# A mixture-of-experts stage whose short last blocks are worked out from raw weights, in two column halves

## The chip, the cores and the metric

The kernel runs on one core of a Trainium2 chip. The metric is the device time of one execution, in microseconds (us); less is better.

## What is computed

The reference is one inference step of a small decoder: 1024 prompt tokens and 64 sample tokens go through an mLSTM layer and a latent-attention layer. Each layer ends with the same kind of channel mixer, and only this mixer is touched here. A shared router gives every one of the 1088 tokens two of 16 experts, so 2176 rows are to be worked out per layer:

```
for each expert e, for its rows x (d = 1024):
    hid = silu(x @ w_gate[e]) * (x @ w_up[e])      # 1024 -> 512
    y   = hid @ w_down[e]                          # 512 -> 1024
out[token] += weight * y                           # two rows per token
```

All is float32. The number of rows of an expert depends on the inputs. Run on the given inputs, the reference's own router gives these counts, experts 0 to 15 in order:

```
layer 0: 151 114 183  90 118 163 153 146 167  80  59 164 158  86 170 174
layer 1: 138 120  80  94 144 104  45 129 221 203 227 243 117 109  99 103
```

## The kernel before

The mixer is `stage_experts` (line 1901), run once per layer. Rows are sorted by expert into blocks of 128 rows; each block is a **slot**. An expert with 151 rows has two slots, the second with 23 real rows. That is 26 slots in layer 0 and 23 in layer 1.

*A product.* A float32 product is made of three fp32r products: weights and inputs are split into an upper part (ACT casts, line 2171 for weights, 2182 for x, 2190 for the hidden rows) and a lower part (DVE subtracts, lines 2263, 2277, 2286), and TensorE (PE) adds upper x upper, upper x lower and lower x upper (lines 2083 to 2085). A slot has 24 such matmuls of 512 columns for gate, 24 for up and 24 for down, 8 transposes of its x (`turn_x`, line 2075) and 4 of its hidden rows (`turn_hidden`, line 2111).

*A slot on PE* (`slot(b)`, lines 2124 to 2132): turn the next slot's x, `up(b)`, first half of `gate(b + 1)`, turn the hidden rows of b, second half of `gate(b + 1)`, `down(b)`. ACT and DVE have the same slot in their own order (lines 2201 to 2216 and 2288 to 2298): on ACT the four pieces of the next gate matrix come first, then the store of the slot before (two copies of PSUM, a drain, one DMA of 512 KB, lines 2192 to 2199), then the two halves of x with two pieces of down after each, the hidden rows, and four pieces of up around silu.

*Weights.* Each matrix (2 MB) has one raw buffer; `load` (line 2010) on the SP queue waits until DVE has lowered the last piece of what was there, then fetches the next. A slot of the same expert as the slot before loads nothing: a table `slot_fresh`, made by DVE in `tables` (line 2420), tells so, and ACT and DVE skip their casts and subtractions (`renew`, lines 2173 and 2266). So 16 times three matrices are loaded per layer. Loads are issued in the order down(b + 1), up(b + 2), gate(b + 3).

*Rows* are gathered by POOL with an indirect DMA into one buffer `xg` (line 2051), which is free again when PE has turned it.

*Loops.* Each engine runs `slots` (line 1994): a loop over all 31 slots that there could be beside the last, with an If that jumps over the body when the slot is not used. The last slot stands behind the loop. Ahead of it DVE works out choices, counts, destinations and tables (lines 2303 to 2434) while PE counts with triangular matmuls (lines 2139 and 2149).

The stage before stores the rows `h2` and fills the part of `yrows` that might stay unwritten (line 1641). The stage after (`stage_combine_latents`, or `stage_combine` in layer 1) gathers `yrows`. The residual rows `g.x` stay in SBUF meanwhile.

The structure that sets the order is the SP queue, with this part of the code:

```
def load(z, b):
    with sp.If(table(sp, g.slot_fresh, b) > 0):
        e = table(sp, g.slot_expert, b) + layer * E
        sp.wait_ge(s_lo[z], b * PIECES + PIECES)
        fetch(z, e)
```

## Time and profile before

| | us |
|---|---|
| median of 3 runs (2448.67 to 2456.14) | 2454.08 |
| the profiled execution, its own time | 2450.45 |
| its span | 2448.8 |
| PE busy in the span | 2236.8 (91%) |
| granted TensorE clock, mean | 0.958 |
| slots of layer 0, from the first slot's start to the last's | 700.8 to 1144.7 |
| slots of layer 1, likewise | 1962.8 to 2355.7 |

The span is taken from the trace of one execution; what lies around it is 1.65 us. A time such as 700.8 counts from the span's start. Busy shares are averages over stages with different limits, so the rows further down are read by stretch: who starts when, and what the row says it waited for (the releaser, behind "<-").

### The profile page before, as it was taken

The numbers are of one execution on the slowest core, as the hardware profiler recorded it, in microseconds if no ns is written. First come the engines' busy times: TensorE is split into PE (matmuls) and PEld (weight loads), VectorE is DVE, ScalarE is ACT, GpSimd is POOL, SyncE is SP. The second block draws the span as 40 slices with busy tenths as digits, with TensorE's granted clock in tenths as the row PEclk, the third lists the DMA queues.
The fourth block names the chain that finished last, engine by engine and source line by source line (L and its number), as shares of the span: only waits on it lengthen the run. The fifth ranks groups of instructions, "written<-read, shape, count | busy, mean of one in ns | idle before, by whom it ended". The sixth has DMA issues, their size and how long they took to land. (4 is left out here: it accounts for less than half of the span.)

```text
span 2448.8 us, 39160 instructions
## 1 busy us (share of the span) xinstructions
PE 2236.8 (91%) x11590; PEld 1675.6 (68%) x11590; DVE 1332.6 (54%) x2251; ACT 1098.1 (45%) x1870; POOL 305.4 (12%) x387
## 2 busy tenths in 40 slices
PE   7999997889689999999799999999989599999974
PEld 4766665667578888887486565656678487888852
DVE  4222312586766756663783444433357677755657
ACT  3211212553346655663543344434332356755645
POOL 0000001670010000000100433000000010000103
PEclk8999998899889999999899999999999699999986
DMA  7566655665468778784556544333351388866956
GB/s 283 173 213 213 218 202 161 173 209 199 157 210 301 289 257 286 275 302 171 156 169 198 180 147 141 94 99 97 101 216 44 128 295 322 325 244 223 328 203 230
DMA packets 194323, 503.98 MB, mean 206 GB/s; under 512 B 19152, under 2 KB 39089, under 8 KB 187696
## 3 DMA queue, kind: packets, MB, share of 16 engines
q1 hardware_dynamic: 165902, 409.88, 49.0%
q0 software_dynamic: 18416, 64.11, 7.4%
q10 hardware_dynamic: 9906, 28.75, 3.3%
q8 instruction: 53, 0.87, 0.1%
q14 instruction: 46, 0.38, 0.0%
HBM read 437.13 MB, written 73.42 MB: 208 GB/s over the span
## 5 line engine op out<-in xcount | busy, mean ns | idle before, releaser
L2263 DVE TENSOR_TENSOR e_wl<-e_raw_gate_up,e_wh 128x1024 fp32r<-128x1024 f32 x256 | 299.7, 1223 | 97.3 <-ACT e_wh L2171 96.5
L2083 PE MATMUL e_psG<-e_wh,e_xh 128*128 128x512 f32 x784 | 315.9, 403 | 11.6 <-issue 7.6
L2085 PE MATMUL e_psG<-e_wh,e_xl 128*128 128x512 f32 x784 | 307.1, 392 | 0.0
L2084 PE MATMUL e_psG<-e_wl,e_xh 128*128 128x512 f32 x784 | 306.2, 391 | 0.0
L2171 ACT CAST e_wh<-e_raw_gate_up 128x1024 fp32r<-128x1024 f32 x256 | 251.2, 1046 | 80.0 <-DMA e_raw_gate_up<-in_e_up 25.3
L2083 PEld LDWEIGHTS e_psG<-e_wh,e_xh 128*128 128x128 f32 x784 | 147.7, 188 | 42.1 <-issue 10.3
L2085 PEld LDWEIGHTS e_psG<-e_wh,e_xl 128*128 128x128 f32 x784 | 147.4, 188 | 32.2
L2084 PEld LDWEIGHTS e_psG<-e_wl,e_xh 128*128 128x128 f32 x784 | 148.0, 189 | 28.3
L2263 DVE TENSOR_TENSOR e_wl<-e_raw_down,e_wh 128x1024 fp32r<-128x1024 f32 x128 | 153.2, 1219 | 15.1 <-ACT e_wh L2171 15.1
L615 PE MATMUL in_ps<-in_w_upper,in_h_upper 128*128 128x512 f32 x384 | 155.5, 405 | 3.1 <-DVE in_h_lower L335 2.7
L2083 PE MATMUL e_psY<-e_wh,e_hh 128*128 128x512 f32 x392 | 154.3, 394 | 2.8 <-DVE e_hl L2286 2.8
L2084 PE MATMUL e_psY<-e_wl,e_hh 128*128 128x512 f32 x392 | 153.7, 392 | 0.0
L2085 PE MATMUL e_psY<-e_wh,e_hl 128*128 128x512 f32 x392 | 153.6, 392 | 0.0
L616 PE MATMUL in_ps<-in_w_lower,in_h_upper 128*128 128x512 f32 x384 | 150.7, 393 | 0.0
L617 PE MATMUL in_ps<-in_w_upper,in_h_lower 128*128 128x512 f32 x384 | 150.4, 392 | 0.0
L2171 ACT CAST e_wh<-e_raw_down 128x1024 fp32r<-128x1024 f32 x128 | 128.1, 1051 | 1.6 <-DMA e_raw_down<-in_e_down 1.6
L2277 DVE TENSOR_TENSOR e_xl<-e_psX,e_xh 128x512 fp32r<-128x512 f32 x98 | 67.2, 688 | 111.0 <-ACT e_xh L2182 111.0
L2182 ACT CAST e_xh<-e_psX 128x512 fp32r<-128x512 f32 x98 | 57.4, 588 | 152.5 <-PE e_psG L2085 123.7
L742 ACT ACTIVATE in_out<-in_ps 128x512 f32<-128x512 f32 (+1 forms) x54 | 32.2, 597 | 206.4 <-PE in_ps L617 201.8
L300 DVE TENSOR_TENSOR in_w_lower<-in_w_raw,in_w_upper 128x512 fp32r<-128x512 f32 x40 | 27.7, 692 | 173.2 <-ACT in_w_upper L294 172.4
L3640 ACT COPY x<-a_psP 128x512 f32<-128x512 f32 (+3 forms) x112 | 52.3, 497 | 127.0 <-PE a_psP L3487 117.0
L1664 PE MATMUL o_ps<-o_w_halves,o_mix_halves 128*128 128x512 f32 (+1 forms) x256 | 102.6, 401 | 3.3 <-DVE o_w_halves L1871 2.2
(616 smaller groups left out, 4490.2 us busy)
## 6 DMA issues: line engine op xcount, KB each, us to landing
e_raw_gate_up<-in_e_gate SPq DMA_DIRECT2D x32, 2048.0 KB, 11.7
e_raw_gate_up<-in_e_up SPq DMA_DIRECT2D x32, 2048.0 KB, 9.3
e_raw_down<-in_e_down SPq DMA_DIRECT2D x32, 2048.0 KB, 7.9
x<-in_ada_w SPq DMA_DIRECT2D x40, 1024.0 KB, 5.4
yrows<-e_y ACTq DMA_DIRECT2D x49, 512.0 KB, 6.7
x<-in_cache SPq DMA_DIRECT2D x64, 320.0 KB
a_pages<-in_cache SPq DMA_DIRECT2D x64, 320.0 KB, 3.5
qkvo<-in_out SPq DMA_DIRECT2D x48, 256.0 KB, 2.3
```

The lines of the kernel that those rows point to most:

```text
L615: T.matmul(dst, up, high[:, k, :], start=(k == 0), stop=False)
L616: T.matmul(dst, up, low[:, k, :], start=False, stop=False)
L617: mm = T.matmul(dst, lw, high[:, k, :], start=False, stop=(k == KD - 1))
L1664: T.matmul(dst, up, wh[k][:, cols], start=(k == 0), stop=False)
L2083: T.matmul(out, upper[:, k, :], wh[:, z, cols], start=k == 0, stop=False)
L2084: T.matmul(out, upper[:, k, :], wl[:, z, cols], start=False, stop=False)
L2085: mm = T.matmul(out, lower[:, k, :], wh[:, z, cols], start=False, stop=k == PIECES * n - 1)
L2171: S.copy(wh[:, z, c * PC:(c + 1) * PC], raw[z][:, c * PC:(c + 1) * PC]).then_inc(s_hi[z], 1)
L2182: S.copy(xh[:, half * 4:half * 4 + 4, :], psX[:, half * 4:half * 4 + 4, :]).then_inc(s_xh, 1)
L2263: V.tensor_tensor(wl[:, z, at], raw[z][:, at], wh[:, z, at].bitcast(F32), ALU.subtract).then_inc(s_lo[z], 1)
L2277: V.tensor_tensor(xl[at], psX[at], xh[at].bitcast(F32), ALU.subtract).then_inc(s_xl, 1)
L3640: S.copy(pT[:, par, lo:hi, :], psP[:, lo:hi, :])
```

## The change

- A slot counts as one only if it has more than 64 rows, or is its expert's first. An expert's last 1 to 64 rows beyond that are a **rest**. For the counts above: 16 slots and 10 rests in layer 0 (experts 0, 2, 5, 6, 7, 8, 11, 12, 14, 15), 20 slots and 3 rests in layer 1 (experts 0, 4, 7). The rest of an expert is worked out beside its last slot.
- A rest's products are plain float32 matmuls that read the raw weights: 64 rows stand as the stationary operand, and the two halves of the output's columns go to the two halves of the PSUM partitions. Gate and up: 8 pairs of matmuls of 256 columns each; down: 4 pairs of 512 columns. There are also 8 transposes of 64 rows of x and 2 of the hidden rows.
- So a raw buffer is also held until the rest's product with it is done: `load` waits for `s_rest[z]`. The gate product of a rest stands in the middle of the down products of the slot before, its up product behind the slot's up, its down product behind the slot's down.
- All slots load weights: `slot_fresh` and the skipping are gone, and the second slot of an expert (four of them, all in layer 1) loads its matrices again. The issue order is gate(b + 1), down(b), up(b + 1).
- A rest's rows are gathered into the same `xg`; the gather of the next slot's x waits until the rest's x is turned. Its result is stored by four DMAs.
- The buffers of a rest lie over the sample rows of `g.x`, which are parked in DRAM and fetched back by the next stage, and over the triangle constants.
- DVE's routing has some more steps, and the tables are made ahead of the token numbers instead of behind them. The loops run over 30 slots. More of `yrows` is filled in the stage before.

The diff, cut to its core:

```diff
-SLOTS = (2 * N + E * (P - 1)) // P
-FULL = 2 * N // P
-
+ROWS = P // 2
+SLOTS = E + (2 * N - 3 * (ROWS + 1)) // P
+PLACES = SLOTS + E + 1
...
-                first = FULL + 2 * t
-                if layer == 0 and first < SLOTS:
-                    more = min(2, SLOTS - first) * P
+                first = E + FILL * t
+                if layer == 0 and first < PLACES:
+                    more = min(FILL, PLACES - first) * P
...
+        parked = g.x[:, PT, :]
+        xr = parked[:, 0:KD * ROWS].rearrange("p (k t) -> p k t", k=KD)
+        hidr, hr = parked[:, HALF:HALF + FE // 2], parked[:, HALF + FE // 2:D]
+        yr = [nc.alloc_sbuf_tensor_at(f"e{layer}_y_rest", [P, FE // 2], F32, offset=g.tri_at), hr]
...
+        psR = ctx.enter_context(nc.psum_tensor(f"e{layer}_psR", [P, 2, FE // 2], F32))
...
+        def rests(eng, b, n):
+
+            return [table(eng, g.slot_halves, b + j) for j in range(n + 1)]
+
+        def with_rest(eng, count, next_count, work):
+
+            with eng.If(next_count > count):
+                work(count)
+            with eng.Else():
+                eng.sem_inc(s_end, 1)
...
             def load(z, b):
-                with sp.If(table(sp, g.slot_fresh, b) > 0):
-                    e = table(sp, g.slot_expert, b) + layer * E
-                    sp.wait_ge(s_lo[z], b * PIECES + PIECES)
-                    fetch(z, e)
-                with sp.Else():
-                    sp.wait_ge(s_raw[z], b * 16)
-                    sp.sem_inc(s_raw[z], 16)
-                sp.drain()
+                e = table(sp, g.slot_expert, b) + layer * E
+                count = table(sp, g.slot_halves, b)
+                sp.wait_ge(s_rest[z], count)
+                sp.sem_inc(s_end, 1)
+                sp.wait_ge(s_lo[z], b * PIECES + PIECES)
+                fetch(z, e)
...
+            used = table(sp, g.slots_used, 0)
+            with sp.Fori(1, SLOTS - 1) as b:
+                with sp.If(used > b + 1):
+                    load(GATE, b + 1)
+                    load(DOWN, b)
+                    load(UP, b + 1)
+                with sp.Else():
+                    sp.sem_inc(s_end, 1)
+            load(DOWN, used - 1)
...
+            def gather_rest(b, h):
+                take(h + (SLOTS - 1), 1)
+                po.wait_ge(s_xt, b + 1)
+                po.sem_inc(s_end, 1)
+                nc.gpsimd.indirect_dma_start(xg[0:ROWS, :], None, g.h2, bass.IndirectOffsetOnAxis(tok[0:ROWS, 1:2], axis=0)
+                                             ).then_inc(s_rx, 16)
...
+                po.wait_ge(s_rt, mine)
+                po.sem_inc(s_ask, 1)
+                gather(tok[:, 0:1])
+                with_rest(po, mine, after, lambda h: gather_rest(b + 1, h))
...
+            def turn_rest(h):
+                pe.wait_ge(s_rx, 16 * h)
+                pe.sem_inc(s_end, 1)
+                for k in range(KD):
+                    mm = T.transpose(psX[:, k, 0:ROWS], xg[0:ROWS, k * P:(k + 1) * P], g.ident[0:ROWS, 0:ROWS])
+                mm.then_inc(s_rt, 1)
+
+            def rest_product(z):
+                for k in range(KD):
+                    for r, c in zip(sides(ROWS), sides(FE // 2)):
+                        mm = T.matmul(psR[r, z, :], xr[:, k, :], raw[z][:, k * FE + c.start:k * FE + c.stop],
+                                      start=(k == 0), stop=(k == KD - 1))
+                mm.then_inc(s_rest[z], 1)
+
+            def gate_rest(h, stored):
+                pe.wait_ge(s_rout, stored)
+                pe.sem_inc(s_end, 1)
+                pe.wait_ge(s_rhf, h)
+                pe.sem_inc(s_end, 1)
+                pe.wait_ge(s_rxf, h)
+                rest_product(GATE)
+
+            def up_rest(h):
+                pe.wait_ge(s_rsilu, h + 1)
+                pe.sem_inc(s_end, 1)
+                pe.wait_ge(s_rout, h)
+                rest_product(UP)
+
+            def turn_rest_hidden(h):
+                pe.wait_ge(s_rhid, h)
+                for j in range(2):
+                    mm = T.transpose(psR[:, 1, j * P:(j + 1) * P], hidr[:, j * P:(j + 1) * P], g.ident[:])
+                mm.then_inc(s_rht, 1)
+
+            def down_rest(h, gates):
+                pe.wait_ge(s_rsilu, gates)
+                pe.sem_inc(s_end, 1)
+                pe.wait_ge(s_rhf, h + 1)
+                out = psR[:].rearrange("p z f -> p (z f)")
+                for f in range(FT):
+                    at = f % 2 * P + f // 2 * ROWS
+                    for r, c in zip(sides(ROWS), sides(HALF)):
+                        mm = T.matmul(out[r, :], hr[:, at:at + ROWS], raw[DOWN][:, f * D + c.start:f * D + c.stop],
+                                      start=(f == 0), stop=(f == FT - 1))
+                mm.then_inc(s_rest[DOWN], 1)
...
             def slot(b):
+                here, soon, later = rests(pe, b, 2)
                 pe.wait_ge(s_xl, b * 2 + 2)
                 turn_x(b + 1)
                 up(b)
+                with_rest(pe, here, soon, up_rest)
                 pe.wait_ge(s_silu, b + 1)
                 gate(b + 1, 0)
                 turn_hidden(b)
+                with_rest(pe, here, soon, turn_rest_hidden)
                 gate(b + 1, 1)
-                down(b)
+                with_rest(pe, soon, later, turn_rest)
+                down(b, range(2))
+                with_rest(pe, soon, later, lambda h: gate_rest(h, here))
+                down(b, range(2, PIECES))
+                with_rest(pe, here, soon, lambda h: down_rest(h, later))
...
+            first = rests(pe, 0, 1)
+            with_rest(pe, *first, turn_rest)
+            with_rest(pe, *first, lambda h: gate_rest(h, h))
...
+            def copy_rest(h):
+                act.wait_ge(s_rt, h + 1)
+                S.copy(xr, psX[:, :, 0:ROWS]).then_inc(s_rxf, 1)
+
+            def silu_rest(h):
+                act.wait_ge(s_rest[GATE], h + 1)
+                S.activation(hidr, psR[:, 0, :], ACT.Silu).then_inc(s_rsilu, 1)
+
+            def copy_rest_hidden(h):
+                act.wait_ge(s_rst, 64 * h)
+                act.sem_inc(s_end, 1)
+                act.wait_ge(s_rht, h)
+                S.copy(hr, psR[:, 1, :]).then_inc(s_rhf, 1)
+
+            def store_rest(h):
+                act.wait_ge(s_rest[DOWN], h + 1)
+                for j in range(2):
+                    S.copy(yr[j][:, :], psR[:, j, :])
+                act.drain()
+                act.sem_inc(s_rout, 1)
+                for z in range(2):
+                    for j in range(2):
+                        at = z * HALF + j * (HALF // 2)
+                        act.dma_start(g.yrows[bass.ds((h + (SLOTS - 1)) * P, ROWS), at:at + HALF // 2],
+                                      yr[j][z * ROWS:(z + 1) * ROWS, :]).then_inc(s_rst, 16)
...
             def slot(b, first=False):
-                now, soon = (table(act, g.slot_fresh, b + j) for j in range(2))
-                renew(GATE, b + 1, soon, b + 1)
+                here, soon, later = rests(act, b, 2)
+                renew(GATE, b + 1, b + 1)
                 if not first:
                     store(b - 1)
                 act.wait_ge(s_xt, b + 2)
                 act.wait_ge(s_xu, b + 1)
                 copy_x(0)
-                renew(DOWN, b, now, b + 1, range(2))
+                renew(DOWN, b, b + 1, range(2))
                 act.wait_ge(s_used[UP], b + 1)
                 copy_x(1)
-                renew(DOWN, b, now, b + 1, range(2, PIECES))
+                renew(DOWN, b, b + 1, range(2, PIECES))
                 copy_hidden(b)
-                renew(UP, b + 1, soon, b + 1, range(2))
+                with_rest(act, here, soon, copy_rest_hidden)
+                renew(UP, b + 1, b + 1, range(2))
                 silu(b + 1)
-                renew(UP, b + 1, soon, b + 1, range(2, PIECES))
+                with_rest(act, soon, later, copy_rest)
+                renew(UP, b + 1, b + 1, range(2, PIECES))
+                with_rest(act, soon, later, silu_rest)
+                with_rest(act, here, soon, store_rest)
...
+            def multiply_rest(h):
+                v.wait_ge(s_rsilu, h + 1)
+                v.sem_inc(s_end, 1)
+                v.wait_ge(s_rest[UP], h + 1)
+                V.tensor_tensor(hidr, hidr, psR[:, 1, :], ALU.mult).then_inc(s_rhid, 1)
+
             def slot(b):
-                now, soon = (table(v, g.slot_fresh, b + j) for j in range(2))
-                renew(GATE, b + 1, soon)
+                here, soon = rests(v, b, 1)
+                lower(GATE, b + 1)
                 lower_x(b + 1, 0)
-                renew(DOWN, b, now, range(1))
+                lower(DOWN, b, range(1))
                 multiply(b)
                 lower_x(b + 1, 1)
-                renew(DOWN, b, now, range(1, 3))
+                lower(DOWN, b, range(1, 3))
+                with_rest(v, here, soon, multiply_rest)
                 lower_hidden(b)
-                renew(DOWN, b, now, range(3, PIECES))
-                renew(UP, b + 1, soon)
+                lower(DOWN, b, range(3, PIECES))
+                lower(UP, b + 1)
...
+                V.tensor_tensor(summed[:], upto[:], rest[:].unsqueeze(1).broadcast_to([P, E, E]), ALU.mult)
+                v.drain()
+                V.tensor_reduce(shift[:], summed[:], AX, ALU.add)
                 V.scalar_tensor_tensor(out=place[:], in0=tmp[:].unsqueeze(1).broadcast_to(sh3), scalar=float(P),
                                        in1=counted, op0=ALU.mult, op1=ALU.add)
                 v.drain()
+                V.scalar_tensor_tensor(out=shift[:], in0=shift[:], scalar=float(SLOTS - 1), in1=ends[:],
+                                       op0=ALU.add, op1=ALU.subtract)
+                V.tensor_tensor(over[:], counted, room[:].unsqueeze(1).broadcast_to(sh3), ALU.is_ge)
+                v.drain()
+                V.scalar_tensor_tensor(out=over[:], in0=over[:], scalar=float(P),
+                                       in1=shift[:].unsqueeze(1).broadcast_to(sh3), op0=ALU.mult, op1=ALU.mult)
+                v.drain()
+                V.tensor_tensor(place[:], place[:], over[:], ALU.add)
...
+            tables()
             v.wait_ge(s_num, 1)
-            V.tensor_scalar(tokens[:], psH[:, 0, 0:SLOTS], float(N), None, ALU.add).then_inc(s_tok, 1)
-            V.tensor_tensor(full[:], ends[:].unsqueeze(1).broadcast_to([P, TABLE, E]),
-                            g.count_up[:].unsqueeze(2).broadcast_to([P, TABLE, E]), ALU.is_le)
-            v.drain()
-            V.tensor_reduce(slotf[:], full[:], AX, ALU.add)
-            v.drain()
-            tables()
+            V.tensor_scalar(tokens[:], psH[:, 0, 0:PLACES], float(N), None, ALU.add).then_inc(s_tok, 1)
```

## Rows read from the trace of the kernel before

**Rows 1.** The page, engines over the span: busy us (share) xinstructions

```profile
PE 2236.8 (91%) x11590; PEld 1675.6 (68%) x11590; DVE 1332.6 (54%) x2251; ACT 1098.1 (45%) x1870; POOL 305.4 (12%) x387
```

**Rows 2.** Stores of slots in ACT's queue, layer 0 and layer 1: duration ns, first and last start

```profile
L2199 ACTq DMA_DIRECT2D yrows<-e_y x26: 343/348/414, 720.8 to 1164.6; - x26
...
L2199 ACTq DMA_DIRECT2D yrows<-e_y x23: 338/343/377, 1982.8 to 2379.8; - x23
```

**Rows 3.** Timeline of PE: start us, us, engine, line [idle before <-releaser]

```profile
700.82 1.03 PE L2075 MATMUL e_psX<-c_ident,e_xg 128*128 128x128 f32 x8
...
718.54 1.03 PE L2075 MATMUL e_psX<-c_ident,e_xg 128*128 128x128 f32 x8
...
1147.21 0.49 PE L2083 MATMUL e_psG<-e_wh,e_xh 128*128 128x512 f32 x1 [2.47 <-issue]
...
1962.81 1.03 PE L2075 MATMUL e_psX<-c_ident,e_xg 128*128 128x128 f32 x8
...
2360.90 0.79 PE L2083 MATMUL e_psG<-e_wh,e_xh 128*128 128x512 f32 x1 [5.16 <-issue]
```

**Rows 4.** Timeline of a fresh slot of layer 1 with fresh neighbours, same columns

```profile
2034.59 1.03 PE L2075 MATMUL e_psX<-c_ident,e_xg 128*128 128x128 f32 x8
2034.97 3.89 ACT L2171 CAST e_wh<-e_raw_gate_up 128x1024 fp32r<-128x1024 f32 x4 [1.00 <-DMA e_raw_gate_up<-in_e_gate]
2040.56 0.59 ACT L2182 CAST e_xh<-e_psX 128x512 fp32r<-128x512 f32 x1 [0.73 <-issue]
2041.18 0.69 DVE L2277 TENSOR_TENSOR e_xl<-e_psX,e_xh 128x512 fp32r<-128x512 f32 x1 [0.18 <-ACT e_xh L2182]
2044.46 2.35 DVE L2263 TENSOR_TENSOR e_wl<-e_raw_down,e_wh 128x1024 fp32r<-128x1024 f32 x2
...
2053.52 1.03 PE L2075 MATMUL e_psX<-c_ident,e_xg 128*128 128x128 f32 x8
```

**Rows 5.** Busy us by engine in 2010 to 2040, then PE clock, DMA share, GB/s

```profile
2010.00:2040.00 30.00, 29.38 (x139) 24.14 (x139) 25.22 (x25) 23.93 (x29) 4.51 (x4) 1.00 1.03 389
```

**Rows 6.** The page, issues of weights: count, KB each, median us to landing

```profile
e_raw_gate_up<-in_e_gate SPq DMA_DIRECT2D x32, 2048.0 KB, 11.7
e_raw_down<-in_e_down SPq DMA_DIRECT2D x32, 2048.0 KB, 7.9
```

**Rows 7.** Timeline of PE in attention, float32 pairs with 64 stationary columns

```profile
1317.57 0.38 PE L3370 MATMUL a_psP<-x,cq_sample 128*64 128x256 f32 x1
1317.79 0.38 PE L3370 MATMUL a_psP<-x,cq_sample 128*64 128x256 f32 x1
...
1693.71 2.80 PE L3461 MATMUL a_psS<-x,a_q_pair 128*64 128x512 f32 x12
1696.44 0.33 PE L3487 MATMUL a_psP<-c_ident,x 128*128 128x128 f32 x1
```

**Rows 8.** ACT between two slots of one expert: timeline, then its queue's table loads

```profile
769.05 1.05 ACT L2171 CAST e_wh<-e_raw_gate_up 128x1024 fp32r<-128x1024 f32 x1 [2.00 <-issue]
...
L1986 ACTq TENSOR_LOAD <-slot_fresh x2: 277/288/299, 767.7 to 768.3; - x2
```

**Rows 9.** PE's queue at skipped slots of the loop: ns, first and last start

```profile
L1998 PEldq COMPARE_BRANCH  x2: 214/214/214, 2354.9 to 2355.8; - x2
```

**Rows 10.** Timeline of POOL, gathers without and with other transfers

```profile
694.66 0.98 POOL L2051 DMA_INDIRECT e_xg<-h,e_tok  x1 [1.60 <-PE e_psX L2075]
699.05 1.05 POOL L2060 COPY e_tok<-e_tokens 128x1 int32 x1 [3.41 <-DMA e_xg<-h,e_tok]
...
2045.49 0.23 POOL L2060 COPY e_tok<-e_tokens 128x1 int32 x1 [7.05 <-DMA e_xg<-h,e_tok]
```

**Rows 11.** Timeline of DVE in the routing of layer 0

```profile
676.47 0.42 DVE L2386 TENSOR_TENSOR e_summed<-e_upto,e_blocks 128x256 f32<-128x256 f32 x1
687.47 0.19 DVE L2444 TENSOR_SCALAR e_tokens<-e_psH 128x32 int32<-128x32 f32 x1 [2.84 <-PE e_psH L2149]
687.58 0.73 DVE L2445 TENSOR_TENSOR e_full<-e_ends,c_count_up 128x560 f32<-128x560 f32 x1
```

More of the change, by code:

```diff
@@ L2244, in _ @@
             last = used - 1
[L2245 to L2249 removed]
+            here, soon = rests(act, last, 1)
+            store(used - 2)
+            renew(DOWN, last, last + 1)
             copy_hidden(last)
+            with_rest(act, here, soon, copy_rest_hidden)
             store(last)
+            with_rest(act, here, soon, store_rest)
+            act.wait_ge(s_rst, soon * 64)
+            act.sem_inc(s_end, 1)
             act.wait_ge(s_st, used * 16 + 32)
@@ L2323, in tables_of_counts @@
                 v.drain()
-                V.memset(least[:, 0, 0:1], -1.0)
             def choose():
@@ L2461, in _ @@
             last = table(v, g.slots_used, 0) - 1
-            renew(DOWN, last, table(v, g.slot_fresh, last))
+            here, soon = rests(v, last, 1)
+            lower(DOWN, last)
             multiply(last)
+            with_rest(v, here, soon, multiply_rest)
             lower_hidden(last)
```

138 lines of the change are left out of this document (81 added, 57 removed).

## The prediction, made before the change was run

> **What bounds the kernel now.** First the page: PE is busy in 91% of the span, every other engine far less [rows 1]. Then the stage itself. ACT's queue stores 26 slots in layer 0 and 23 in layer 1 [rows 2]; the same numbers come out of the reference's counts, rounded up to blocks of 128, so the counts hold here. From slot to slot PE takes 718.54 - 700.82 = 17.72 us [rows 3]. This is 72 matmuls and 12 transposes without a gap: 8 transposes take 1.03, some 0.8 without the modelled tail of the last, 4 take 0.4, two changes between kinds 0.2, and 16.3 / 72 = 0.227 is left for a matmul, 2.7 for half a gate product. From the first slot's start to the end of the last down product but one, layer 0 takes 1147.21 - 2.47 - 700.82 = 443.9 and layer 1 takes 2360.90 - 5.16 - 1962.81 = 392.9.
>
> What is next behind PE shows where three slots with new weights (fresh slots, by the table's name) follow each other: a slot there takes 2053.52 - 2034.59 = 18.93, because gate's raw weights landed late (ACT waited 1.00 for the DMA), and the lower half of x, which PE needs, comes 2041.18 + 0.69 - 2034.97 = 6.9 after ACT's first cast of gate [rows 4]. The DMA engines are then full, at 389 GB/s [rows 5]. A fresh slot moves three matrices of 2.10 MB and two times 0.52 MB of rows, 7.34 MB; 7.34 / 389 is 18.9 us. So a slot costs 17.7 by PE and 18.9 by DMA once all are fresh.
>
> **What goes and what comes, on PE.** 49 slots become 36, and 13 rests come. A rest's pairs run side by side in this trace: the same shape of 256 columns steps by 1317.79 - 1317.57 = 0.22 per pair, and 12 matmuls of 512 columns are followed by the next instruction after 1696.44 - 1693.71 = 2.73, or 0.455 for a pair with the change of shape in it [rows 7]. So gate 8 x 0.22 and 0.2 for a change of shape = 2.0, up 2.0, down 4 x 0.455 = 1.8 and 0.2 = 2.0, x's transposes 1.1, hidden ones 0.3: 7.4 us. If that were all, a slot saved (17.7) would be paid with 7.4.
>
> **What it adds as waits.** A rest holds raw buffers that were free early. I count in time from PE's start of a slot.
>
> Gate's matrix for slot b + 1 is asked for when the rest's gate product of b is done. That product is followed by half a down, 2.7, so it is asked for at -2.7, and a matrix takes 7.9 to land when little else is under way [rows 6]: 5.2. Where slot b - 1 had a rest of its own, the request is earlier by its down product, 2.0, but ACT is late: store_rest waits for that product, copies two times 256 columns (0.35 each, estimated from 0.59 for 512 [rows 4]) and drains, 1.0 with the wait, and issues four DMAs, 0.35 each by [rows 2] and some 0.1 of address work, 1.7; then the loop's end and two table loads take 2.00, and a third load one step of 0.6 more, 767.7 to 768.3 [rows 8], less 0.3 of the drain counted before. Sum 5.0. So in both cases gate's casts begin at about 5.1 instead of 0.4, and half of x is ready at 5.0 + 6.9 = 11.9. PE, done with turn, up and up_rest at 0.8 + 5.4 + 2.0 = 8.2, waits 3.7. Half a gate, 14.6; hidden transposes, 15.0. The rest's hidden rows wait on DVE, where multiply_rest is queued behind three pieces of down: 2044.46 + 2.35 - 2034.97 = 11.8 after the first cast [rows 4], plus 0.5: 17.4. Transposed 17.7, second half of gate 20.4, down 5.4, down_rest 2.0: **27.8** for a slot with a rest. With a rest in the next slot too, 1.1 and 2.0 more: **30.9**. A slot without a rest behind one with: 11.9 + 2.7 + 0.4 + 2.7 + 5.4 = **23.1**, and **26.2** if the next has one. A slot without a rest ahead of one with: 17.7 + 3.1 = 20.8, and 1.0 for the next x: its gather now starts only after turn_rest and takes 4.4 alone (694.66 to 699.05), 7.05 and its issue beside other transfers [rows 10]: **21.8**. Anything else: **18.9**.
>
> Behind ACT's four DMA issues are queued gate's casts, store(b - 1) and x's copies; SP's queue is in order, so down(b) and up(b + 1) are late with gate, but down lands at about 10.8, just ahead of its casts, and up is needed later. They cost nothing unless gate gets earlier; then down is late next.
>
> **The sum.** Layer 0, 15 slots ahead of the last: five of 30.9, four of 27.8, two of 26.2, two of 21.8, two of 23.1 = 407.9, against 443.9: -36.0. Layer 1, 19 slots: three of 27.8, three of 23.1, two of 21.8, eleven of 18.9 = 404.2, against 392.9: +11.3. That layer saves only three slots, and the four second slots load again.
>
> Ahead of slot 0, in both layers a slot with a rest: x's gather starts at 701.9, behind turn_rest, and takes 4.7; the slot begins at 706.6, not 700.82: +5.8 each, 11.6.
>
> The end of the loop: a skipped slot costs PE 0.92, 2354.9 to 2355.8 [rows 9]; 6 are skipped in layer 0 now and 9 in layer 1, of which 2.47 and 5.16 are seen as idle [rows 3]. It becomes 15 and 11, as PE's queue is ahead by no more than now: +8.3 and +1.8. In layer 0's last slot come 2.0 of down_rest and 1.1 of its store and other rest work (up_rest stands where PE waits anyway): +3.1. Together 13.2.
>
> Routing: a second product and sum over 256 columns, 0.42 each [rows 11], and four small steps with drains, 1.5; the token table over 48 instead of 32 places, 576 more columns at the 0.73 / 560 of [rows 11], 0.75; the tables, 4.1 in all (two old and two new passes of 0.73 and 1.2 of small steps), move ahead of the token numbers, where 2.84 were idle: 1.3. Sum 4.4 per layer, 8.8. What DVE saves behind the tokens is hidden by the gather. Other edits: the larger fill, the parked rows and their return run beside work, 1 us in all, between 0 and 4 (a 2 MB transfer ends the stage before later if its cover is gone).
>
> Sum: -36.0 + 11.3 + 11.6 + 13.2 + 8.8 + 1 = **+9.9**. From the execution's own 2450.45 that is 2460.4; the median of the runs is 3.6 above that execution, so I say 2464. The bounds of the price taken at least surely, gate's first cast: between 3.4 (ACT's queue runs ahead of its copies) and 9 (a landing of 11.7, the median of gate's loads [rows 6], behind a rest). It acts in 19 slots: -32 to, in the nine with a landing to wait for, +35.
>
> **The Trainium skill against a row.** The rows show 389 GB/s over 30 us. The Trainium skill's page "DMA: Bandwidth & Descriptors", section "Where 436 GB/s comes from", says that between HBM and SBUF about 358 GB/s is the limit. By that, a fresh slot would be 20.5 us, an estimate from the page, and the sum some 18 higher. The trace disagrees with it for this stretch; the sum goes by the row.
>
> **The rivals.**
> A, not slower: gate's casts begin early enough. The point is 5.1 - 9.9 / 19 = 4.6: from there down the change wins. At 2.7, which holds if ACT's loads and DMA issues overlap what it waits for and gate lands at once, it is -2.4 x 19 = -46 and 2418. For it: ACT's queue does run ahead where it is not held (casts of up and gate follow each other). Against: it is held here by a wait and a drain. 0.30.
> B: eleven fresh slots in a row don't keep 389 GB/s, which the trace shows for 30 us only. At a tenth less, 1.9 x 11 = 21: 2485. Against: rate and pitch agree in [rows 4, 5]. 0.10.
> C: jumps. A skipped slot takes 0.92, of which two compares are 0.43 [rows 9]. PE's slot body grows by more than half and has six Ifs; where its queue has lost its lead after a wait, 0.5 to 0.9 could stand open in each of 34 slots: +24 and 2488. Against: 25 returns in layer 0 show no gap now. 0.07. The Trainium skill's page "Runtime: NRT & Kernel Launch", section "Instruction fetch mechanics", says that a taken branch out of the fetched window stalls the sequencer for a fetch; the 0.92 agrees with it.
> D: the pairs go one after the other: 5.4 for each of 13 rests, +70, 2534. The pairs in [rows 7] speak against it. 0.03.
> E, it doesn't do what it says (another number of rests, weights not loaded): the counts match [rows 2], so this is nearly nothing and has no chance of its own.
>
> **The numbers.** The forecast, waits as worked out, has 0.50 and spans 2446 to 2490. A measurement of this kernel can tell about 0.3%, 7 us, from no change: 0.15 of the forecast's 0.50 and a little of A lie within it. Faster 0.29, same 0.17, slower 0.54. The range takes in most of A's better side and B and C: 2415 to 2500.
>
> **What would show it.** Slots of about 31, 28, 26, 23 and 19 us in PE's timeline; gate's first cast at 5 us in slots with a rest or behind one, and PE waiting for DVE's x (line 2277) and then for multiply_rest; pairs at 0.22; DMA at 1.0 and 389 GB/s in the second half of layer 1; a gap near 11 us ahead of layer 0's last slot; routing longer by 4.4. Wrong if casts of gate begin before 4.6, if rest slots take 25, or if fresh slots leave 18.9.

## The result and the profile after

The changed kernel takes 2562.59 us (median of four runs, 2556.92 to 2564.43), the kernel before 2454.93 beside it: 1.044 times as long, interval 1.0423 to 1.0456. So the sign of the forecast was right and its size far off: 2464 with a range up to 2500.

The profiled execution has a span of 2561.2 us, 112.4 more. The page of the changed kernel, PE's busy time and the granted clock in 40 slices:

```profile
span 2561.2 us, 39115 instructions
PE 2212.0 (86%) x11668; PEld 1586.4 (62%) x11669; DVE 1358.6 (53%) x2270; ACT 1121.2 (44%) x1905; POOL 311.3 (12%) x388
PEclk9999998999689999998899999999999689899987
```

PE is busy for 86% of the span where it was 91% [rows 1]: PE now waits. PE's groups of the raw products in the changed kernel (count; busy, mean; idle time before):

```profile
L2167 PE MATMUL e_psR<-e_raw_gate_up,x 128*64 128x256 f32 x832 | 98.9, 392 | 3.9 <-ACT x L2309 3.9
```

There are 13 rests, as worked out. But 832 records are 64 for each, and the code writes 32 matmuls for gate and up together. Each float32 matmul shows as two records.

One slot with a rest, in layer 0, PE's timeline (start, duration, engine, line, operation, in brackets the idle time before it and what ended it):

```profile
969.59 1.09 PE L2120 MATMUL e_psX<-c_ident,e_xg 128*128 128x128 f32 x8
...
976.10 3.67 PE L2167 MATMUL e_psR<-e_raw_gate_up,x 128*64 128x256 f32 x32
982.96 0.49 PE L2128 MATMUL e_psG<-e_wh,e_xh 128*128 128x512 f32 x1 [3.18 <-DVE e_xl L2412]
983.29 0.40 PE L2129 MATMUL e_psG<-e_wl,e_xh 128*128 128x512 f32 x1
...
984.24 0.63 PE L2129 MATMUL e_psG<-e_wl,e_xh 128*128 128x512 f32 x1
984.67 0.63 PE L2130 MATMUL e_psG<-e_wh,e_xl 128*128 128x512 f32 x1
...
987.39 0.60 PE L2206 MATMUL e_psH<-c_ident,e_hid 128*128 128x128 f32 x4
988.15 0.44 PE L2188 MATMUL e_psR<-c_ident,x 128*128 128x128 f32 x2 [0.16 <-DVE x L2427]
...
996.97 3.65 PE L2199 MATMUL e_psR<-e_raw_down,x 128*64 128x512 f32 x16
1000.55 1.09 PE L2120 MATMUL e_psX<-c_ident,e_xg 128*128 128x128 f32 x8
```

A raw product takes 3.6 us, not 2.0. PE waits for the lower half of x, as forecast; behind the wait the pitch of matmuls is 984.67 - 984.24 = 0.43 instead of the 0.227 worked out from [rows 3], so half a gate product takes 987.39 - 982.96 = 4.43 us instead of 2.7. The granted clock of this stretch is 0.62 on average (982.9 to 987.4 us): most of it went at the lower of the clock's two levels (1.2 GHz), and before it PE had stood for 3.18 us. The slot takes 31.0 where the forecast said 27.8.

ACT in the changed kernel: gate's casts of four slots (those that start at 714.51, 781.89, 969.59 and 1000.55), then a rest's stores and gate's first cast around the start of the slot at 898.62.

```profile
725.61 3.88 ACT L2281 CAST e_wh<-e_raw_gate_up 128x1024 fp32r<-128x1024 f32 x4 [10.60 <-DMA e_raw_gate_up<-in_e_gate]
...
788.51 3.89 ACT L2281 CAST e_wh<-e_raw_gate_up 128x1024 fp32r<-128x1024 f32 x4 [8.97 <-DMA e_raw_gate_up<-in_e_gate]
...
975.96 3.89 ACT L2281 CAST e_wh<-e_raw_gate_up 128x1024 fp32r<-128x1024 f32 x4 [5.61 <-issue]
...
1006.77 3.89 ACT L2281 CAST e_wh<-e_raw_gate_up 128x1024 fp32r<-128x1024 f32 x4 [5.46 <-issue]
```
```profile
898.74 0.37 ACT L2324 COPY e_y_rest<-e_psR 128x256 f32<-128x256 f32 x1 [6.14 <-PE e_psR L2199]
899.01 0.38 ACT L2324 COPY x<-e_psR 128x256 f32<-128x256 f32 x1
899.63 0.52 ACTq L2330 DMA_DIRECT2D yrows<-e_y_rest  x1
900.33 0.48 ACTq L2330 DMA_DIRECT2D yrows<-x  x1
900.98 0.53 ACTq L2330 DMA_DIRECT2D yrows<-e_y_rest  x1
901.66 0.55 ACTq L2330 DMA_DIRECT2D yrows<-x  x1
904.78 1.99 ACT L2281 CAST e_wh<-e_raw_gate_up 128x1024 fp32r<-128x1024 f32 x2 [5.39 <-issue]
```

Gate's first cast comes 11.1, 6.6, 6.4, 6.2 and 904.78 - 898.62 = 6.2 us behind the slot's start; the forecast said 5.1. In the first two the load came last, in the others ACT's own issues. A DMA issue is followed by the next after 0.65 to 0.70 here, not 0.45.

The second half of layer 1, ten slots in a row with neither a rest nor one before them, ran as forecast or better (the eleventh such slot stands earlier in the layer). Nine of the ten lie in 2279 to 2445 us of the changed kernel; its engines and DMA there (columns: PE, PEld, DVE, ACT, POOL busy, clock, DMA share, GB/s); [rows 5] is its like:

```profile
2279.00:2445.00 166.00, 161.91 (x758) 132.00 (x757) 147.84 (x144) 130.62 (x162) 20.98 (x17) 1.00 1.03 394
```

Slots of 17.7 to 18.9 us and 394 GB/s. Where the 112.4 us lie, from slot starts in PE's timeline, with the forecast in brackets: slots +26.8 in layer 0 (-36.0) and +32.4 in layer 1 (+11.3); ahead of the first slots +13.7 and +14.6 (10.7 each, with 4.4 of routing and half of the 1 us of other edits); behind the last slot but one +20.1 (11.4) and +4.8 (1.8). So 83.9 of the miss of 102.5 lie in slots.

### The profile page after: what moved, and what is told of

The parts are those of the page before. It is cut to its first block and busy times, and to the rows that moved or that the text cites. A ratio compares the mean times of both kernels' runs of the same rounds, so it can differ in the third digit from the quotient of the medians.

```text
span 2561.2 us, 39115 instructions
## 1 busy us (share of the span) xinstructions
PE 2212.0 (86%) x11668; PEld 1586.4 (62%) x11669; DVE 1358.6 (53%) x2270; ACT 1121.2 (44%) x1905; POOL 311.3 (12%) x388
## 5 line engine op out<-in xcount | busy, mean ns | idle before, releaser
L2406 DVE TENSOR_TENSOR e_wl<-e_raw_gate_up,e_wh 128x1024 fp32r<-128x1024 f32 x288 | 336.0, 1221 | 296.7 <-ACT e_wh L2281 296.3
L2281 ACT CAST e_wh<-e_raw_gate_up 128x1024 fp32r<-128x1024 f32 x288 | 283.4, 1045 | 215.3 <-DMA e_raw_gate_up<-in_e_gate 101.6
L2128 PE MATMUL e_psG<-e_wh,e_xh 128*128 128x512 f32 x576 | 252.4, 438 | 123.0 <-DVE e_xl L2412 99.9
L2129 PE MATMUL e_psG<-e_wl,e_xh 128*128 128x512 f32 x576 | 241.5, 419 | 0.0
L2130 PE MATMUL e_psG<-e_wh,e_xl 128*128 128x512 f32 x576 | 240.6, 418 | 0.0
L2128 PE MATMUL e_psY<-e_wh,e_hh 128*128 128x512 f32 x288 | 114.9, 399 | 2.4 <-DVE e_hl L2421 2.4
L2130 PE MATMUL e_psY<-e_wh,e_hl 128*128 128x512 f32 x288 | 112.3, 390 | 0.0
L2129 PE MATMUL e_psY<-e_wl,e_hh 128*128 128x512 f32 x288 | 112.2, 390 | 0.0
L615 PEld LDWEIGHTS in_ps<-in_w_upper,in_h_upper 128*128 128x128 f32 x384 | 72.4, 189 | 48.5 <-ACT in_out L742 23.2
L2167 PE MATMUL e_psR<-e_raw_gate_up,x 128*64 128x256 f32 x832 | 98.9, 392 | 3.9 <-ACT x L2309 3.9
```

What stands on the lines that cost most here:

```text
L615: T.matmul(dst, up, high[:, k, :], start=(k == 0), stop=False)
L2128: T.matmul(out, upper[:, k, :], wh[:, z, cols], start=k == 0, stop=False)
L2129: T.matmul(out, upper[:, k, :], wl[:, z, cols], start=False, stop=False)
L2130: mm = T.matmul(out, lower[:, k, :], wh[:, z, cols], start=False, stop=k == PIECES * n - 1)
L2167: mm = T.matmul(psR[r, z, :], xr[:, k, :], raw[z][:, k * FE + c.start:k * FE + c.stop], start=(k == 0), stop=(k == KD - 1))
L2281: S.copy(wh[:, z, c * PC:(c + 1) * PC], raw[z][:, c * PC:(c + 1) * PC]).then_inc(s_hi[z], 1)
```

## The experiments

Two theories at first. **T**: the rest's products cost PE twice what I took. **W**: what was mis-sized are the waits, buffers held and ACT late, and the products matter little. Each run is set against 2562; the kernel before, beside them, had medians of 2450 to 2455.

**Price of a rest as a whole** (the last rows of 13 experts are left out):

```
-V.tensor_scalar(g.slot_halves[:], restf[:], 1.0, None, ALU.add)
+V.tensor_scalar(g.slot_halves[:], restf[:], 0.0, 1.0, ALU.mult, ALU.add)
```

> The changed kernel with the table of rests set to 1 everywhere, so that no slot does any rest work on any engine; the last rows of 13 experts are left out. Slots (36), loads, the loop's end and the routing stay. Both theories: what is left are 34 slots at 17.7 (PE) to 18.9 us (DMA) plus heads and tails, so about 2561 - 13 x 22 = 2275 us. It tells the price of one rest with all that it drags along: I expect (2561 - this) / 13 = 22 us, against the 12 us of PE work by theory T (a float32 product is two passes) and about 10 of waits. If the slots stay above 20 us without rests, both theories are wrong and it is the loads of all slots or the new branches.

Measured: 2276.19 us. By the spans, (2561.2 - 2276.8) / 13 = 21.9 us for a rest. Its engines and DMA over ten slots of layer 0:

```profile
785.00:966.00 181.00, 179.24 (x838) 145.86 (x837) 163.75 (x161) 146.60 (x180) 20.10 (x19) 1.00 1.04 403
```

Ten slots in 181.86 us (785.09 to 966.95) at 403 GB/s: loading in every slot costs 0.5 us of a slot and no more. Within the slots, then, neither the branches nor the loads are the cause.

The run says one thing more. The kernel before has a span of 2448.8; less 13 slots of 17.72 it would be 2218.4, and this run's is 2276.8. So 58 us of the 112 come with the change even where no rest is worked out: some 29 in the 34 slots (0.5 in most, 5.8 and 6.7 in the layers' first), 15 in gaps ahead of the two last slots (13.14 and 9.54 where there were 2.47 and 5.16), the remainder ahead of the first slots and in the next stage. The other 54 are 13 times the difference between 21.9 and 17.7.

**Half of each product** (half of the contraction is left out), and **one side of each pair** (all of the right half but its first matmul is left out):

```
-for k in range(KD):          # and f in range(FT) in down_rest
+for k in range(KD // 2):     # and f in range(FT // 2)
```
```
-for r, c in zip(sides(ROWS), sides(FE // 2)):   # in down_rest likewise
+for r, c in list(zip(sides(ROWS), sides(FE // 2)))[:1 if k else 2]:
```

> The changed kernel with each of the rest's three products over half of its contraction (the other half is left out): 16 instead of 32 records in gate_rest and up_rest, 8 instead of 16 in down_rest. Theory T (PE's own work: 3.65 us each, gate_rest and down_rest in full on the path, up_rest where PE waits for x anyway, and raw buffers asked for earlier): 1.8 + 1.8 = 3.6 us less per rest, 13 rests, -47 us: about 2515. Theory W (the cost is that ACT comes late with gate's casts behind store_rest and that raw buffers are held; the products themselves fill time that PE would wait): under 15 us less, 2547 or more.

> The changed kernel with the right-hand column half of each rest's product left out but for its first matmul (so half of each result is wrong); the left-hand half is whole. If the two matmuls of a pair run side by side, each group takes as long as before (gate_rest 3.6, down_rest 3.6 us) and the time stays within 5 us of 2561. If they go one after the other (rival D), the products halve as in the run with half the contraction and the time falls by about 47 us. Theory T says side by side, two passes each: 32 records become about 18, with the same 0.22 us per step.

Measured: 2499.43 us and 2564.87 us. The PE records of line 2167 (gate's and up's raw products) from 700 to 1185 us, first the changed kernel, then one side left out, then half the contraction:

```profile
L2167 PE MATMUL e_psR<-e_raw_gate_up,x 128*64 128x256 f32 x608 | 71.5, 389 | 2.1 <-ACT x L2309 2.1
```
```profile
L2167 PE MATMUL e_psR<-e_raw_gate_up,x 128*64 128x256 f32 x342 | 71.4, 391 | 2.1 <-ACT x L2309 2.1
```
```profile
L2167 PE MATMUL e_psR<-e_raw_gate_up,x 128*64 128x256 f32 x320 | 39.8, 392 | 2.6 <-ACT x L2309 2.5
```

342 records take as long as 608, and 320 over half the contraction take 56% of it. So the two matmuls of a pair do run side by side (rival D is out), and a step of the contraction costs two records of 0.22 us one after the other, called two passes here. Half the products gave 63 us, 4.9 per rest, where T said 3.6 and W at most 15 us in all.

**Next to no products** (all steps of the contraction but the first are left out):

```
-for k in range(KD):
+for k in range(1):           # and f in range(1)
```

> The changed kernel with each of the rest's products cut to its first step of the contraction (one pair for gate and up, one pair for down; the other seven and three are left out). Everything else of a rest stays: gathers, transposes, copies, silu, the four stores, all waits and branches, and raw buffers held until the products are done. Half of the contraction gave 62 us. Theory T: going on to an eighth and a quarter takes another 3.6 x 3/8 x 2 (gate and up, the latter only where PE doesn't wait for x) and 3.6 / 4 for down: 2.2 to 3.6 per rest, and a little more because gate's matrix is asked for earlier: 2455 to 2465. What then still lies between this run and the 2276 without rests, some 180 us or 14 per rest, is waits and fixed work, which would be more than the products. If it falls to 2400 or less, the products are nearly the whole price.

Measured: 2474.98 us, 88 less than 2562 and still 199 above the kernel without rests: 15.3 us a rest that are not its products. That was more than I expected, and T alone falls with it. In this run PE waited longer instead (5.7 to 6.2 us for x in slots with a rest next to others, where it was 3.0 to 4.0): part of the products stood in time that PE would wait.

**ACT's stores later**: store_rest of slot b - 1 behind gate's casts in slot b (and likewise in the last slot).

```
 renew(GATE, b + 1, b + 1)
 if not first:
+    with_rest(act, table(act, g.slot_halves, b - 1), here, store_rest)
     store(b - 1)
...
 with_rest(act, soon, later, silu_rest)
-with_rest(act, here, soon, store_rest)
```

> The changed kernel with ACT's store_rest (wait for down_rest, two copies, drain, four DMA issues) moved from the end of its slot to behind gate's casts of the next one, beside the store of the whole rows. Theory W: gate's first cast behind a rest comes at 3 us or less after the slot's start where it came at 6 (unless the load itself is late), the wait of PE for x shrinks by 3 in up to 12 slots: about -30 us, 2532. Theory T: the same mechanism, but it is the smaller part of the miss; where the load is what comes last (gate asked for only after gate_rest) nothing is won, so -15 to -30. If nothing changes, ACT's place for store_rest doesn't set the pace.

Measured: 2543.07 us, -19.5. A slot behind one with a rest, with no rest of its own and none in the next, falls from 26.4 to 27.0 us to between 23.8 and 25.3, since gate's casts no longer wait for ACT. Where a rest follows a rest nothing is won, but not because the load comes last. Gate's first cast there does come 3.3 to 3.6 us earlier, 2.8 to 3.0 behind the slot's start where it was 6.2 to 6.4, and the load is what it waits for. But the stores now stand between gate's casts and x's. ACT in the slot that starts at 965.30, and x's cast in the changed kernel's slot that starts at 969.59:

```profile
968.10 3.89 ACT L2281 CAST e_wh<-e_raw_gate_up 128x1024 fp32r<-128x1024 f32 x4 [8.82 <-DMA e_raw_gate_up<-in_e_gate]
...
977.31 0.59 ACT L2288 CAST e_xh<-e_psX 128x512 fp32r<-128x512 f32 x1 [0.70 <-issue]
```
```profile
981.51 0.58 ACT L2288 CAST e_xh<-e_psX 128x512 fp32r<-128x512 f32 x1 [0.70 <-issue]
```

x's cast comes 12.0 behind the slot's start, and 11.9 in the changed kernel: ACT has the same work ahead of it in either order.

**Gate's raw product earlier**, ahead of down, or behind its first quarter, both with the late store:

```
-down(b, range(2))
+down(b, range(1))            # in the first of the two: not at all
 with_rest(pe, soon, later, lambda h: gate_rest(h, here))
-down(b, range(2, PIECES))
+down(b, range(1, PIECES))
```

> The changed kernel with store_rest late as in the run before (2543) and gate_rest ahead of the whole down product instead of in its middle. Gate's matrix is asked for 2.7 us earlier, so that less of its landing is waited for: where the load came last, gate's casts come up to 2.7 earlier (-15 to -25 over some 10 slots). Against that, PE meets gate_rest before ACT has copied the rest's rows: 1.4 to 2.1 us open in 13 rests, +18 to +27. So about the same as the late store alone, 2543 within 12. Theory W expects a clear gain, 2520 or less, theory T that the 12 us of PE work per rest stand whatever the order.

> As the run before it, but gate_rest behind the first quarter of down (1.36 us) instead of ahead of it or in its middle: the copy of the rest's rows is covered for the most part, and the load is asked for 1.4 us earlier than in the changed kernel. Both theories: a little better than the late store alone (2543), by 5 to 15: 2532.

Measured: 2537.12 (2532.56 to 2538.79) and 2537.99 (2529.82 to 2540.29): the same as each other, 5 to 6 better than the late store alone.

**Skipped slots** cut off (loops to 19, for these counts only), on the changed kernel and on the last order:

```
-with eng.Fori(0, SLOTS - 1) as b:     # SP's and ACT's own loops likewise
+with eng.Fori(0, 19) as b:
```

> The changed kernel with its loops over slots ending at 19 instead of 30 (enough for the 16 and 20 slots of these inputs only), so 11 skipped slots fewer in each layer: 4 are left in layer 0, none in layer 1. With 0.92 us for a skipped slot on PE, and idle of 13.32 us in layer 0 and 9.59 us in layer 1 ahead of the last slot in the changed kernel's trace: at most 10.1 + 9.6 = 20 us less, 2542; at least 10 less if ACT's or SP's skipped slots end later than PE's anyway. If the gap stays, it wasn't the skipped slots.

> The kernel of the run before it with loops that end at 19: the sum of both, 2532 - 20 = 2512. If theory T is right, no order of these pieces comes near the kernel before (2452): 2276 without rests and 13 x 12 us of PE work alone are 2432, and each rest still drags some us of waiting. Below 2470 would say that the waits were the main part.

Measured: 2549.57, -13 (expected -20), and 2519.8, -18. The gap ahead of the last slot falls from 13.32 to 3.48 us in layer 0 and from 9.59 to nothing in layer 1, where PE then waits 3.75 instead of 0.86 us for DVE's hidden rows. That is 16.5 of gaps, of which the run won 13; where the other 3.5 went isn't shown. 11 iterations fewer took 9.84 off layer 0's gap, 0.89 each.

**A rest's store DMAs issued by SP** instead of ACT, between the loads of down and up, on top of the run before (2519.8):

```
-act.dma_start(g.yrows[...], yr[j][...]).then_inc(s_rst, 16)
...
 load(DOWN, b)
+with_rest(sp, *rests(sp, b - 1, 1), store_rest)
 load(UP, b + 1)
```

> The kernel with the late store, gate_rest behind a quarter of down and loops to 19 (2520), with the four store DMAs of a rest issued by SP between the loads of down and up instead of by ACT. ACT gets 2.6 to 3.2 us back between gate's casts and the copy of x in 12 slots behind a rest; PE waits there for x for 2.2 us and runs its next 9 matmuls at half its clock, 1.7 us. So -2 to -4 in 12 slots, -24 to -48: 2484. The kernel before stands at 2452 to 2455. Theory T: not below it, since the products and 36 slots alone are 2432 and the ends of the layers and the first slots add waits. If it does come below, the design pays once the waits are gone.

Measured: 2532.79, 13 worse, not 24 to 48 better. The slots take as long as before: from the first slot's start to the start of the last one in the loop, layer 0 takes 419.0 us where it took 420.0 in the run before (2519.8), and layer 1 395.2 where it took 395.1. ACT's time is not free to win there, since with its issues gone it came to the casts of down before the load had landed, and waited for it 11 times, 32.8 us together in layer 0, where it had waited 7 times, 19.0 us. The loss lies behind layer 0. SP's queue is in order, and the next stage's first transfers now stand behind the last rest's stores. SP's first transfer and PE's first product with weights of that stage, in the run before and in this one:

```profile
1185.11 0.36 SPq L2072 DMA_DIRECT2D l_rows<-in_ln_g  x1
...
1207.17 1.27 PE L2960 MATMUL l_psL<-l_raw,l_bias 128*33 128x320 f32 x2 [1.52 <-DVEq L3158]
```
```profile
1206.81 0.36 SPq L2083 DMA_DIRECT2D l_rows<-in_ln_g  x1
...
1224.38 1.25 PE L2966 MATMUL l_psL<-l_raw,l_bias 128*33 128x320 f32 x2 [9.95 <-DMA l_raw<-in_w_kv_a]
```

The transfers start 21.7 later, PE 17.2. Of the 12.2 us by which the spans differ, 10.5 lie between the start of the last slot in layer 0's loop and layer 1's first slot. So the 13 us are the price of the new place of the last stores, not of the slots; the run was not repeated with these left on ACT.

**The clock.** In nearly all slots with a rest or behind one, the half gate product behind PE's wait takes 4.4 to 5.3 us. Ten identity matmuls (`keep_warm`) fill the wait in slots with a rest:

```
 rest_product(UP)
+keep_warm(T, g, psH[:, 0, 0:P], 10)
```

> The changed kernel with ten 128 x 128 matmuls of the identity behind the rest's up product, on a bank nobody reads then, and nothing else: PE does them where it waits for x's lower half in the 12 slots that have a rest (waits of 2.96 to 4.0, and 7.4 and 6.0 in the first slot of a layer). Six such took 0.83 us as x6 records for three matmuls, so ten are about 2.8. Theory C2 (the clock): the half gate product behind such a wait takes 4.4 to 5.3 us instead of 2.7 because the wait brings the granted clock down to the lower level; with the wait filled it takes 2.7 to 2.9, 1.7 less in about 10 slots: 2562 - 17 = 2545. If the clock isn't a term of its own, the time stays at 2562 or rises by what the matmuls take.

Measured: 2572.07, not 2545: 10 worse. The slot shown above, with the identity matmuls (PE's timeline; the slot starts at 975.38):

```profile
981.89 3.67 PE L2167 MATMUL e_psR<-e_raw_gate_up,x 128*64 128x256 f32 x32
985.49 2.50 PE L77 MATMUL e_psH<-c_ident 128*128 128x128 f32 x20
988.65 0.49 PE L2128 MATMUL e_psG<-e_wh,e_xh 128*128 128x512 f32 x1 [0.66 <-DVE e_xl L2413]
...
991.49 0.60 PE L2207 MATMUL e_psH<-c_ident,e_hid 128*128 128x128 f32 x4
993.85 0.44 PE L2189 MATMUL e_psR<-c_ident,x 128*128 128x128 f32 x2 [1.76 <-DVE x L2428]
994.27 0.49 PE L2128 MATMUL e_psG<-e_wh,e_xh 128*128 128x512 f32 x1
...
998.70 0.40 PE L2128 MATMUL e_psY<-e_wh,e_hh 128*128 128x512 f32 x1
```

The half gate product is back to 2.84 us, and PE now waits 1.76 for the rest's hidden rows, which DVE multiplies behind two pieces of down. The second half gate product, behind that wait, then takes 998.70 - 994.27 = 4.43 instead of 2.86. So it goes in 7 of the 10 slots where PE waits there, 1.4 to 1.6 us each, 11 together, about the loss. The slow clock had covered a wait. The changed kernel itself has a pair of slots that shows it, the ones that start at 898.62 and 934.06:

```profile
911.78 0.63 PE L2128 MATMUL e_psG<-e_wh,e_xh 128*128 128x512 f32 x1 [2.96 <-DVE e_xl L2412]
...
916.98 0.44 PE L2188 MATMUL e_psR<-c_ident,x 128*128 128x128 f32 x2 [0.17 <-DVE x L2427]
...
947.30 0.49 PE L2128 MATMUL e_psG<-e_wh,e_xh 128*128 128x512 f32 x1 [3.05 <-DVE e_xl L2412]
...
952.50 0.44 PE L2188 MATMUL e_psR<-c_ident,x 128*128 128x128 f32 x2 [1.73 <-DVE x L2427]
```

The first half gate product takes 4.44 us in the one and 2.87 in the other, and the wait for the rest's hidden rows makes up the difference: the slots take 35.44 and 35.53. So a third theory: **a slot with a rest is set by ACT's and DVE's chain from gate's cast to multiply_rest, and PE's clock shows only once that is out of the way.** It says that DVE's order alone wins nothing and both together win what each alone does not:

```
+with_rest(v, here, soon, multiply_rest)
 lower(DOWN, b, range(1, 3))
-with_rest(v, here, soon, multiply_rest)
```

> The changed kernel with DVE's multiply_rest ahead of the two pieces of down instead of behind them, so that the rest's hidden rows are ready 2.35 us earlier; no identity matmuls. If the low clock and the wait for multiply_rest cover each other: PE reaches turn_rest_hidden at the same time as before, having run the half gate product at half its clock, and only its wait of 0.16 us goes: -2 us, 2560 within 5.

> Both together: multiply_rest first and ten identity matmuls behind the rest's up product. If the two covered each other, the pair wins what neither wins alone: half gate product 2.85 instead of 4.4 to 5.3 us, no wait of 1.76 behind it: 1.5 to 1.7 us in 10 to 11 slots, -17, 2545, where the matmuls alone gave 2572 and the order alone about 2560. If it is the chain on DVE and ACT in some other place, it stays at 2560 to 2572.

Measured: 2560.0 and 2546.66 us. Against 2562.59 each change alone gives -3, which the spread of the runs doesn't tell from nothing, and +10; both together give -16, where the sum would be +7. So the third theory holds for slots with a rest. With both, PE's timeline of that slot is 28.57 us long instead of 30.96:

```profile
961.23 1.09 PE L2120 MATMUL e_psX<-c_ident,e_xg 128*128 128x128 f32 x8
...
974.39 0.49 PE L2128 MATMUL e_psG<-e_wh,e_xh 128*128 128x512 f32 x1 [0.54 <-DVE e_xl L2413]
977.26 0.60 PE L2207 MATMUL e_psH<-c_ident,e_hid 128*128 128x128 f32 x4
...
989.80 1.09 PE L2120 MATMUL e_psX<-c_ident,e_xg 128*128 128x128 f32 x8
```

**How near the design comes.** Seven identity matmuls on the best order (without multiply_rest first), and then everything that helped:

> The best order so far (late store, gate_rest behind a quarter of down, loops to 19; 2520) with seven identity matmuls behind the rest's up product, about 2 us, where PE waits 2.1 to 2.8. There 5 of the 12 slots with a rest still had a half gate product at 4.4 or 5.3 us instead of 2.85: 5 x 1.6 = -8, 2512. It is to show how near the design can come to the kernel before (2450 to 2455) with the waits and the clock mended but the products as they are.

> Late store, gate_rest behind a quarter of down, loops to 19, multiply_rest first, and seven identity matmuls: all that was found to help. 2520 without the last two; the pair gives 1 to 1.6 in some 8 slots: 2508. The kernel before is at 2452 to 2455, and what is left, 232 us above the 2276 without rests, is 17.8 per rest, 12 of them PE's own work.

Measured: 2522.03, no gain, for the reason just shown, and 2509.97. That is 53 below the changed kernel and 2.3% (2.1 to 2.5) above the kernel before. In it PE stands 2.2 to 2.9 us for ACT's copy of the next rest's rows, in the five slots of layer 0 that have a rest and another ahead.

No version here beats the kernel before. How little room there is: 36 slots without rests are 2276, and 13 times PE's own work for a rest, 3 x 3.6 + 0.7 + 0.4 = 11.9 us, bring that to 2431. That is some 20 below the kernel before, for all the waits that 13 rests bring, with 13 to 18 more to gain from shorter loops. That no order of the pieces gets there is not shown.

## Why the prediction was right in sign and wrong in size

The chain of waits it named is what happened: raw buffers and ACT's stores make gate late, PE waits for x's lower half, and what 13 fewer slots save is eaten up. What failed is the price of a pair of raw matmuls, with smaller misses behind it. Its points one by one.

- **Counts, slot types, fresh slots**: right. 36 slots, 13 rests, the types and their numbers; slots without rests at 17.7 to 18.9 (18.9 forecast), so rival B is out. The limit of 358 GB/s that the Trainium skill's page "DMA: Bandwidth & Descriptors" gives (section "Where 436 GB/s comes from") was passed here for 166 us, at 394.
- **"Gate 8 x 0.22 and 0.2 = 2.0 ... down 2.0"**: the step that failed first. The 0.22 in [rows 7] is the pitch of a record, and a float32 matmul has two, one after the other. So the runs showed 3.65 us instead of 2.0 for each product. Gate's and down's stand on the path: 2 x 1.65 x 13 = +43 us, of it 38 in the slots (23 products). Up's stands where PE would wait, as was said. This could be read before: the x12 in [rows 7], from which I took 0.455 for a pair, are six matmuls in the code of that line, three pairs, so 0.91 for a pair.
- **"Gate's casts begin at about 5.1"**: measured 6.0 to 6.4 where ACT came last. The chain in ACT was right, its steps too short: four DMA issues and what lies between them take 2.6 where 1.7 was said. In the 17 slots with a rest or behind one, the layers' first left out, it came at 6.0 to 7.6, 6.4 on average: 1.3 in 17 slots, +22. In the first slots of the layers it was later still (11.1 in layer 0, behind a load; in layer 1 half a gate product began 4.2 later than forecast): +10. A's point of 4.6 was not reached in any of the 19.
- **A term that was missing: the clock.** Behind PE's wait half a gate product takes up to 5.28. In slots with a rest it costs next to nothing, since PE would wait for multiply_rest, at 11.8 + 0.5 behind gate's cast as the forecast has it (measured 988.15 - 975.96 = 12.2). In the seven slots behind a rest without one of their own there is no such wait, and it adds 1.7 to 2.6 each: +15 by the rows. Filling their waits was not tried.
- Together 38 + 22 + 10 + 15 = 85, where the slots were off by 83.9. That these meet is partly luck: the eleven slots without rests took 202.0, 5.9 less than forecast, and the four ahead of a rest 91.0, only 3.8 more than forecast though gate's product alone adds 1.65 to each, so that 7.6 more must lie in the other slots. Most of it would be that matmuls step by 0.23 to 0.24 instead of 0.227: the slot with a rest of 27.8 is 31.0 by 1.65 for down, 1.2 for the cast and about 0.3 for pitches.
- **Heads and tails**: +18.6 beyond the forecast. Ahead of the first slots 6.9. Gate's raw product took longer there (5.3 us in layer 0, 6.4 to the slot's start in layer 1) than the gather that the forecast took for the limit; with the product cut to its first step, PE waits for that gather and the slots start 1.6 and 2.7 sooner behind the product's start. Layer 0's end: all 15 skipped slots stand open (13.32, said 11). That isn't the rests' doing: without them the gap is 13.14. The next stage is late by the rest of the 8.7.
- **Rival C**, jumps: out. Slots take 18.2 us without rests, and in the changed kernel PE stands behind "issue" at no slot's start or inside one, but for 1.06 us at layer 1's first. **Rival D** as put, pairs one after the other, is out by the run with one side; but its price, 5.4 for each rest, is near what the second pass costs, and its 2534 was the nearest to the result of all cases. The row it was dismissed by was the one that was misread.

## What to carry to other kernels

Count the records of a shape against the matmuls in the code before using their pitch as a price: a float32 matmul counted double here. Before filling or shortening a wait, ask which chain ends next; two terms that cover each other (a slow clock and a late DVE) show no gain until both are taken, and the sum of single experiments misleads. A tail worked out beside whole blocks has to be cheaper than the block it saves with all that it drags along: here 21.9 us against 17.7, and 58 us for the rest of the change on top. When work moves to another queue, look at what stands behind it there, at the end of the loop too: the slots were as long as before, and the next stage started 17 us late.

## What the runs showed of the hardware

- A float32 matmul of 256 or 512 columns shows as two records and takes two passes (0.22 and 0.45 us each). With 0.91 us for 512 columns it takes four times the 0.227 of an fp32r matmul. Two of them whose outputs lie on different halves of the PSUM partitions overlap fully: 342 records took 71.4 us, 608 took 71.5.
- Behind a wait of 3.18 us the next matmuls went at a pitch of 0.43 us, the lower level, for most of half a gate product (4.43 us, granted clock 0.62); behind a wait of 0.66 us with identity matmuls ahead of it at 0.23 (2.84 us, granted clock 1.00). Of two waits in the changed kernel nearly alike, 2.96 and 3.05 us, one was followed by 4.44 and the other by 2.87.
- 403 GB/s were kept up over ten slots, 181 us, at a DMA share of 1.04.
- Four DMA issues in a row on ACT's queue follow each other by 0.65 to 0.70 us and take some 0.5 each; the single issue of a slot's store takes 0.34 to 0.41.
- A skipped iteration of the loop costs PE 0.87 to 0.89 us: PE stood 13.32 for 15 of them ahead of layer 0's last slot, 3.48 for 4.
